# Differential attention ahead of the last keys' norms, and the first mixer's mask in the decay rows

## What is computed

```python
def forgetting_attention(q, k, v, f_logit):
    c = jnp.cumsum(jax.nn.log_sigmoid(f_logit), axis=1)
    ...
        s = jnp.einsum('bhtd,bshd->bhts', qi, k) * scale
        s = s + ci[..., :, None] - c[:, :, None, :]
        s = jnp.where(kpos[None, :] <= qpos[:, None], s, -jnp.inf)
        p = jax.nn.softmax(s, axis=-1)
        return jnp.einsum('bhts,bshd->bthd', p.astype(v.dtype), v)
...
def diff_attention_group(q, k, v, z, q_gain, k_gain, lq1, lk1, lq2, lk2, out_gain, lambda_init):
    q = rmsnorm(q.reshape(b, t, DF_HEADS, 2, DF_HEAD_QK), q_gain) * (DF_HEAD_QK ** -0.5)
    k = rmsnorm(k.reshape(b, t, DF_HEADS, 2, DF_HEAD_QK), k_gain)
    ...
        s = jnp.einsum('bqhcd,bkhcd->bhcqk', q_blk, k).astype(jnp.float32)
        p = jax.nn.softmax(jnp.where(mask, s, neg), axis=-1)
        wts = p[:, :, 0] - lam * p[:, :, 1]
        return jnp.einsum('bhqk,bkhv->bqhv', wts.astype(v.dtype), v)
    ...
    o = rmsnorm(o, out_gain).astype(jnp.float32) * (1.0 - lambda_init)
    return (o * jax.nn.silu(z)).astype(z.dtype)
```

## Time and profile before

| | us |
|---|---|
| median of 3 runs | 921.55 |
| lowest, highest | 918.61, 921.67 |
| the profiled execution | 918.34 |
| its span, first to last instruction | 916.7 |
| TensorE busy | 900.9 |
| VectorE busy | 551.6 |
| ScalarE busy | 292.1 |

### The profile page before, as it was taken

How to read it: one execution, slowest core, us unless ns; L and a number is a source line. 1 busy time by engine, 2 the same in 40 slices (tenths; PEclk the granted TensorE clock), 3 DMA queues, 4 the chain that set the end, 5 groups by cost and what they waited for, 6 DMA issues and landing times.

```text
span 916.7 us, 13260 instructions
## 1 busy us (share of the span) xinstructions
PE 900.9 (98%) x4499; PEld 730.7 (80%) x4499; DVE 551.6 (60%) x968; ACT 292.1 (32%) x596; POOL 72.3 (8%) x138
## 2 busy tenths in 40 slices
PE   8999999999999999999999999999999999999998
PEld 7887776778888888888888888888888897567877
DVE  7247456355877777767743434497777463775654
ACT  6234456523322222222210101443330112454710
POOL 0000000000010010001000001000000000000000
PEclk9999999999999999999999999999999999999999
DMA  8756443254766556655665655578456222212554
GB/s 276 246 188 196 159 128 115 83 160 135 235 200 196 183 190 198 198 193 184 195 198 191 198 184 186 181 224 258 150 149 194 67 86 92 92 62 77 168 194 145
DMA packets 50213, 154.76 MB, mean 169 GB/s; under 512 B 9564, under 2 KB 10860, under 8 KB 50040
## 3 DMA queue, kind: packets, MB, share of 16 engines
q1 hardware_dynamic: 22320, 75.70, 26.1%
q0 software_dynamic: 19008, 69.21, 23.1%
q10 hardware_dynamic: 8840, 9.23, 3.1%
HBM read 149.63 MB, written 4.49 MB: 168 GB/s over the span
## 4 chain that ended last, share of the span: by engine, by line
PE 91%; DVE 3%; issue 2%; DMA 2%; ACT 2%; DVEq 0%; SPq 0%; POOLq 0%; ACTq 0%
PE bank L654 77%; PE bank L713 1%; DMA HI<-wstream 1%; PE bank L1091 1%; PE bank L1071 1%; PE bank L792 1%; PE bank L816 1%; PE bank L1002 1%; PE bank L988 1%; PE bank L806 1%; DVE LO L1621 1%; DMA RAW<-wstream 1%; PE bank L1082 1%; PE bank L795 0%; DVE SQ L1603 0%
## 5 line engine op out<-in xcount | busy, mean ns | idle before, releaser
L654 PE MATMUL bank<-GH,HI 128*128 128x512 f32 (+1 forms) x724 | 292.5, 404 | 1.6 <-issue 1.6
L654 PE MATMUL bank<-GH,LO 128*128 128x512 f32 (+1 forms) x724 | 282.3, 390 | 0.0
L654 PE MATMUL bank<-GL,HI 128*128 128x512 f32 (+1 forms) x724 | 282.0, 389 | 0.0
L1621 DVE TENSOR_TENSOR LO<-RAW,HI 128x1024 fp32r<-128x1024 f32 x88 | 107.5, 1222 | 115.7 <-DMA HI<-wstream 114.8
L654 PEld LDWEIGHTS bank<-GH,HI 128*128 128x128 f32 x724 | 136.5, 188 | 34.1 <-issue 9.0
L654 PEld LDWEIGHTS bank<-GH,LO 128*128 128x128 f32 x724 | 136.3, 188 | 29.0
L654 PEld LDWEIGHTS bank<-GL,HI 128*128 128x128 f32 x724 | 136.8, 189 | 23.9
L636 POOL DMA_DIRECT2D HI<-wstream x132 | 69.8, 529 | 820.2 <-PE bank L654 810.2
L1333 ACT ACTIVATE YC<-AB,PAR 128x512 f32<-128x512 f32 x44 | 36.0, 818 | 140.7 <-DVE AB L1768 140.5
L654 PE MATMUL bank<-AH,HI 128*128 128x512 f32 x176 | 69.3, 394 | 0.0
L654 PE MATMUL bank<-AH,LO 128*128 128x512 f32 x176 | 69.0, 392 | 0.0
(11 more groups left out here) (309 smaller groups left out, 1178.0 us busy)
## 6 DMA issues: line engine op xcount, KB each, us to landing
RAW<-wstream SPq DMA_DIRECT2D x135, 512.0 KB, 3.7
HI<-wstream POOLq DMA_DIRECT2D x132, 512.0 KB, 5.0
X<-x_t SPq DMA_DIRECT2D x8, 256.0 KB, 7.6
NCB<-out_t ACTq DMA_DIRECT2D x4, 512.0 KB, 3.8
out_t<-X ACTq DMA_DIRECT2D x8, 256.0 KB, 5.7
XR<-out_t ACTq DMA_DIRECT2D x8, 256.0 KB, 3.5
out_t<-XR SPq DMA_DIRECT2D x7, 256.0 KB, 3.8
EG<-out_t ACTq DMA_DIRECT2D x1, 1024.0 KB, 6.1
```

What stands on the lines that cost most here:

```text
L654: mm = pe.matmul(out, a, b, start=(first and n == 0), stop=(last and n == 2))
L1621: dve.tensor_tensor(LO[:, u % RING, :], RAW[:, u % RING, :], HI[:, u % RING, :].bitcast(F32), ALU.subtract).then_inc(unit_split, 1)
```

## The change

1. *Mask.* The fourth matmul of the scores goes, with IDF and CSF and ScalarE's two copies that made them. NCB now holds, for each of two heads and two pairs by turns, eight blocks of 128: the transfer lands the four key blocks at places 1, 3, 5, 7 (two transfers of 256 KB a pair, in pieces of 512 bytes), and VectorE writes the block without mask at 0 and blocks with the mask subtracted at 2, 4, 6 (item "bias (p, 0)") and in place at 7 ("bias (p, 1)"). The maxima read a strided choice of these places. The transfer of pair 2 and 3 waits until the maxima of the pair before last are taken.
2. *Order of the first mixer.* Slot 0 stands ahead of the last three quarters of qk 3, slot 1 behind its last quarter, the ring step of that tile behind its remainder (lowqk 3). The new items shift the fills: slots 2, 3, 6, 7, 10 and 11 stand one quarter or two earlier, C 0 and "split 5" ahead of the last quarter of u 2 and qk 6, and lowqk 7 ahead of gate 1.
3. *Order of the second mixer.* X, Y, Z and W of the last blocks stand one eighth earlier. Two eighths of z 0 stand ahead of the last sums, scores 0 behind one more; kn 2 stands in slot 3 behind B 1, kn 3 in slot 4 behind B 2, each with an eighth ahead of it. The list then reads:

```diff
@@ -112,6 +112,16 @@
+def _last_norms(slots):
+
+    slots[0] = [("z", (0, 0)), ("P", 0), QUERIES_KEYS[-1], ("qr", 1)] + slots[0]
+    slots[3].append(("P", 1))
+    slots[3].append(("kn", 2))
+    slots[4].append(("P", 2))
+    slots[4].append(("kn", 3))
+    return slots
...
-            if item[0] in ("A", "B") and item not in without:
+            if item[0] in ("A", "B", "P") and item not in without:
                 order.append(left.pop(0))
-            order.append(item)
+            if item[0] != "P":
+                order.append(item)
...
@@ -195,6 +206,8 @@
+        if n % 4 >= 2 and n < 12:
+            slot.append(("bias", (n // 4 + 1, n % 4 - 2)))
...
-    return (first[:3] + norms[:2] + first[3:4] + [("ncb", 0)] + _merge(first[4:13], norms[2:]) + first[13:] + [("lowqk", 3)]
-            + part(0, 4, products(4, 7)) + part(4, 8, _merge(products(7, 10), scaled))
-            + part(8, 12, [("gelu", 0)] + last[:7] + [("gate", 0)] + last[7:] + [("gate", 1), ("lowqk", 7), ("gate", 2)])
+    return (first[:3] + norms[:2] + first[3:4] + [("ncb", 0)] + _merge(first[4:13], norms[2:]) + first[13:16] + [("bias", (0, 0)), ("bias", (0, 1))] + slots[0][:1] + first[16:18] + slots[0][1:] + first[18:]
+            + _spread([[slots[1][0], ("lowqk", 3)]] + [[x] for x in _flat(slots[1:4])[1:]], products(4, 7)) + part(4, 8, _merge(products(7, 10), scaled))
+            + part(8, 12, [("gelu", 0)] + last[:7] + [("gate", 0)] + last[7:] + [("lowqk", 7), ("gate", 1), ("gate", 2)])
...
-    + _prepare(2, QUERIES_KEYS[43:])
-    + [("qr", 1)] + _eighths(range(1))[:3] + [("kn", 2)] + _eighths(range(1))[3:4] + [("kn", 3)]
-    + _with_products(_attention(4), _eighths(range(5))[4:36], [])
+    + _prepare(2, QUERIES_KEYS[43:-1])
+    + _with_products(_last_norms(_attention(4)), _eighths(range(5))[1:36], [])
...
                         r = slice(64 * e, 64 * e + 64)
-                        pe.matmul(PS[2 + e][:, 0:w], q[r, 4 + p, P * i:P * (i + 1)], k[r, p, 0:w],
-                                  start=(part == 0), stop=False)
-                for e in range(2):
-                    pe.matmul(PS[2 + e][:, P * i:w], IDF[:, :], CSF[:, :], start=False, stop=True).then_inc(s_made, 1)
+                        mm = pe.matmul(PS[2 + e][:, 0:w], q[r, 4 + p, P * i:P * (i + 1)], k[r, p, 0:w],
+                                       start=(part == 0), stop=(part == 2))
+                        if part == 2:
+                            mm.then_inc(s_made, 1)
...
-                    act.dma_start(NCB[:, 2 * n:2 * n + 2, :],
-                                  out_t[2 * n:2 * n + 2, :].unsqueeze(0).to_broadcast([P, 2, T]))\
-                       .then_inc(scratch_landed, 16)
+                    elif n >= 2:
+                        act.wait_ge(max_made, 8 * (n - 1))
+                    for e in range(2):
+                        head = out_t[2 * n + e, :].rearrange("(j c) -> j c", c=P)
+                        act.dma_start(NCB[:, n % 2, e, 1:8:2, :], head.unsqueeze(0).to_broadcast([P, NB, P]))\
+                           .then_inc(scratch_landed, 16)
...
-                dve.wait_ge(scratch_landed, 16 * (n // 4 + 1))
+                S = S.rearrange("p (j c) -> p j c", c=P)
+                bias = NCB[:, n // 4 % 2, e, (slice(2, 3), slice(0, 5, 4), slice(0, 7, 3), slice(1, 8, 2))[n % 4], :]
+                dve.wait_ge(biased, 3 * (n // 4 + 1))
...
+            def mask_bias(p, part):
+
+                rows = NCB[:, p % 2, :, :, :]
+                diagonal = CAUSAL[:, 384:512].unsqueeze(1)
+                if part == 0:
+                    dve.wait_ge(scratch_landed, 32 * (p + 1))
+                    dve.tensor_copy(rows[:, :, 0, :], rows[:, :, 1, :]).then_inc(biased, 1)
+                    dve.tensor_tensor(rows[:, :, 2:7:2, :], rows[:, :, 1:6:2, :],
+                                      diagonal.unsqueeze(1).to_broadcast([P, 2, 3, P]), ALU.subtract).then_inc(biased, 1)
+                else:
+                    dve.tensor_tensor(rows[:, :, 7, :], rows[:, :, 7, :], diagonal.to_broadcast([P, 2, P]), ALU.subtract)\
+                       .then_inc(biased, 1)
```

More of the change, by code:

```diff
@@ L61 @@
 STORED_NCB, STORED_ROWS, STORED_BETA, STORED_NT, STORED_XS = (16 * n for n in (1, 2, 3, 11, 12))
-LANDED_ROWS, LANDED_BETA, LANDED_MS, LANDED_XI = (16 * n for n in (5, 6, 7, 15))
+LANDED_ROWS, LANDED_BETA, LANDED_MS, LANDED_XI = (16 * n for n in (9, 10, 11, 19))
 FREED_VA, FREED_DFV = NB, 2 * NB
@@ L302, in _ring @@
             out.append(("ring", U_KQV + n + RING - 1))
-        if what in ("qk", "u") and n[1] == 3:
+        if (what, n) == ("qk", (3, 3)):
+            continue
+        elif (what, n) == ("lowqk", 3):
+            out.append(("ring", U_QK + 3 + RING - 1))
+        elif what in ("qk", "u") and n[1] == 3:
             out.append(("ring", U_QK + MIX1_UNITS.index((what, n[0])) + RING - 1))
@@ L384, in build @@
         FR = place("FR", [P, 3, T], F32, arena + 64 * KB)
-        NCB = place("NCB", [P, 8, T], F32, arena + 80 * KB)
+        NCB = place("NCB", [P, 2, 2, 8, P], F32, arena + 80 * KB)
         VA = place("VA", [P, NB, 512], F32, arena + 96 * KB)
@@ L389, in build @@
         SGB = place("SGB", [P, 4, P], F32, arena + 112 * KB)
-        IDF = place("IDF", [P, P], F32R, arena + 114 * KB)
-        CSF = place("CSF", [P, P], F32R, arena + 114 * KB + 512)
         assert arena + 115 * KB <= 229368, arena
@@ L1680, in biased_max @@
                 S = PS[2 + e][:, 0:w]
[L1681 removed]
+                S = S.rearrange("p (j c) -> p j c", c=P)
+                bias = NCB[:, n // 4 % 2, e, (slice(2, 3), slice(0, 5, 4), slice(0, 7, 3), slice(1, 8, 2))[n % 4], :]
+                dve.wait_ge(biased, 3 * (n // 4 + 1))
                 dve.wait_ge(s_made, 2 * n + e + 1)
[L1683 removed]
+                dve.tensor_tensor_reduce(S, S, bias, -1.0, 3e38, ALU.add, ALU.min,
                                          MX1[:, c:c + 1]).then_inc(max_made, 1)
+            def mask_bias(p, part):
[9 more added lines that the diff above has]
+                       .then_inc(biased, 1)
             for what, n in MIX1_ORDER:
@@ L1705, in _ @@
                     dve.tensor_tensor(rest, full, top.bitcast(F32), ALU.subtract).then_inc(qk_split, 1)
+                elif what == "bias":
+                    mask_bias(*n)
                 elif what == "A":
```

7 lines of the change are left out of this document (1 added, 6 removed).

## The result

| | us |
|---|---|
| kernel before, median of 20 executions | 917.77 (915.81 to 923.40) |
| changed kernel, median of 20 executions | 921.42 (919.09 to 923.81) |
| ratio, 95% interval | 1.0032 (1.0019 to 1.0044) |
| profiled execution of the changed kernel, its span | 923.08, 921.4 |

The change costs 2.9 us by the ratio (1.7 to 4.0) and 3.65 by the medians, and the forecast was a gain of 1.3. The time itself, 921.42, lies inside the range, yet that is luck: the three runs at hand beforehand stood 3.8 us above the median of twenty.

A forecast was written before the change was run, and what follows sets the result against it. TensorE, busy 98% of the span, was taken as the bound. First mixer -2.6 and second mixer +1.3 summed to -1.3 us: 917.0 for the profiled execution, 920.2 for the three-run median; range 914.6 to 924.5.

The forecast's parts named there:

- VectorE ... has no gap after it: First mixer, slots 8 to 13: VectorE works without idle from about 141.45 us, so slot 12's maxima start at 156.4.
- Rival D: Clock falls more often at new TensorE waits, including ahead of slot 13: slower, 923.3 us with two falls; chance 0.18.
- The 0.95 us of slots 8 to 13: First mixer: slot 12's maxima start at 156.4 instead of 157.40, bringing slot 13's scores 0.95 us earlier, a gain.
- the 1.45 us of slots 0 to 7: First mixer's first eight slots: 2.2 us gained from dropped mask products, less a new 0.75 us wait at slot 1.
- 0.27: First mixer: each dropped pair of mask products saves 0.27 us where TensorE sets the pace; slot 15 counts one such gain.
- slot 9's exponentials don't move with TensorE: First mixer: these start at 139.87 us behind the gelu's table load, and stay there when TensorE runs earlier.
- The second mixer: Start of attention: new waits of 4.1 and 1.3 us at the spreads against 4.2 removed; with new falls, 1.3 us lost.
- the fall at 773: Second mixer, sums of the last key tile: clock at 0.76 over 7 us; avoiding it was credited with 1.7 us.
- 0.3 for new falls: Second mixer: a new wait of 3 to 4 us may bring another clock drop, costing 0.3 us (0 to 1.7).
- B: Second mixer: the spreads don't stall, so all 4.2 us are gained; 914.7 us, chance 0.15.
- C: First mixer: the mask was free and VectorE's added 6.2 us lie on the chain, so no gain; 922.8 us, chance 0.17.
- E: Second mixer: attention starts ahead of the norms only on TensorE's list, ScalarE holding the spreads back; no own time or chance.

The follow-up runs named there:

- experiments 7: Changed kernel with unit 24's ring step behind slot 13's maxima, two gate products ahead of the last sums, both spreads ahead of the first scores: 917.86 us, ratio 0.9993.
- experiment 9: Kernel before with the change's mask and first-mixer order, unit 24's ring step moved behind slot 13's maxima, second mixer as before: 915.46 us, ratio 0.9965.
- 10: Kernel before with the change's first mixer, unit 24's ring step behind slot 13's maxima, and only two gate products ahead of the last sums: 915.39 us, ratio 0.9963.
- experiment 2: Changed kernel with the second mixer's order put back as before, leaving the mask and the first mixer's new order: 919.00 us, ratio 1.0009 to before.
- experiment 5: Changed kernel with only unit 24's ring step on VectorE moved from behind gate 2 to behind slot 13's maxima: 918.10 us, ratio 1.0000 to before.
- 6 before, step moved: Kernel before with only unit 24's ring step on VectorE moved from behind gate 2 to behind slot 13's maxima: 917.18 us, ratio 0.9994.
- experiment 11: Kernel before without the first mixer's pairs of mask products and nothing in their place, so it computes something else: 916.04 us, ratio 0.9972.
- experiment 12: Kernel before with the second mixer's new order, but spread kn 2 behind slot 4 and kn 3 behind slot 6: 922.73 us, ratio 1.0040.
- experiment 1: Kernel before with only the second mixer's new order: 921.20 us against 918.01, ratio 1.0043.
- 4: Kernel before with the change's mask, first mixer's other order left, both bias steps of pair 0 behind the last remainder: 921.89 us, ratio 1.0043.
- 8: Kernel before with the change's first-mixer order, mask products left on TensorE and no bias steps: 917.55 us, ratio 0.9999.

## Why the forecast was wrong, step by step

*The failing step: "VectorE ... has no gap after it", slots 8 to 13.* I added the 1.55 us of bias to VectorE's busy time and took it that nothing else would hold it. The list puts the ring step of unit 24 between gate 2 and slot 12's maxima, and I had counted its work but not its load. Before, that load was issued at 150.30 and landed 4.5 us later, and the step came at 156.26, 1.4 us after the landing. The change brings VectorE to the step at 154.8, while the load, issued when qk 7 ends, moves ahead by 0.6 us only (149.66). An unchanged landing would still have come 0.6 us before the step, so the change didn't make the wait by itself: it took the load's slack from 1.4 us to 0.6, and in this profile the load came 7.0 us after the issue. The issues of the two kernels in the stretch from 145 to 160 us (last number: us to landing), first before, then after:

```profile
HI<-wstream POOLq DMA_DIRECT2D x1, 512.0 KB, 4.5
```

```profile
HI<-wstream POOLq DMA_DIRECT2D x1, 512.0 KB, 7.0
```

In the fourteen profiles it took 4.5 to 7.0 us. In eleven of them, experiments 7, 9 and 10 with the new first mixer included, it took 4.5 to 5.5; the three slow ones are the changed kernel (7.0), experiment 2 (6.8) and experiment 5 (6.0). Only in these three does an instruction-fetch packet of 16 KB, 0.95 us long, fall into the load's way from issue to landing (at 153.6, 153.2 and 152.5 us). So the slow landings go with the fetch; that the fetch causes them is argued from these traces, and no run moves it. What the runs do show is the step's place: moved, the wait and the fall of the clock behind it are gone. Rival D had the place, "the time ahead of slot 13", and its stated price, but not its cause, and I gave it 0.18.

*A second fault, in the sum.* The 0.95 us of slots 8 to 13 came from 157.40 against 156.4, both counted from the start of the span. So it is the whole lead at slot 13, and the 1.45 us of slots 0 to 7 are in it; the sum adds the two. By its own terms the first mixer's gain was 0.95 + 0.27 = 1.2 us and not 2.6, and the whole came to about nothing. The premise behind it, that slot 9's exponentials don't move with TensorE, didn't hold either. They start 1.40 us earlier than the 139.87 of the earlier trace rows, as much as slot 8's scores:

```profile
138.47 0.47 ACT L1305 ACTIVATE P<-bank,SM 128x256 f32<-128x256 f32 x1
```

The distances between the starts of scores show what each stretch gave, in us, without what lies ahead of 70 us:

```text
                              from the product at 70     from slot 8
                              to slot 8                  to slot 15
before                        59.00                      39.99
changed kernel                57.97                      42.78
2 first mixer only            57.97                      42.56
5 changed, step moved         57.97                      38.68
6 before, step moved          58.99                      39.06
9 first mixer, step moved     58.00                      38.67
11 no mask products           57.47                      39.40
```

From slot 8 to slot 15 the forecast has 1.2 us of gain, and the changed kernel loses 2.8. With the step moved it gains 1.3, of which the move alone gives 0.9 in the kernel before, so 0.4 are the change's. With the step in its place and its load in time, slot 12's maxima would start at 154.8 + 1.14 = 155.9, an estimate from the changed kernel's rows: 1.5 us ahead of the earlier trace rows, of which 1.4 stood at slot 8. So even then this term would have been near 0.

*Slots 0 to 7.* Forecast: 2.2 gained, 0.75 lost, net 1.45. Measured 1.03 from the product at 70 us to slot 8: the wait at slot 1 was 0.49, and the pair is worth 0.19 instead of 0.27 (experiment 11), so 1.52 - 0.49. By the Trainium skill, page "TensorE: Matmul & The Clock Gate", section "Back-to-back issue gap", its formula for an isolated matmul makes an estimated 0.11 a pair, which the prediction took; the same section says that this under-counts at small sizes and puts 81 ns on a 128-column matmul in a stream, an estimated 0.16 a pair and 2.6 us for the 32. The distance between the two kernels, 0.19 a pair over eight slots and 2.2 to 2.6 us for the whole, lies close to that second figure, and the row's 0.27 was too much. The pair's row and the next one's were not the whole of what removing the pair changes, so the price of a removal is better read as the distance between two kernels. The bias work was sized well; VectorE's groups in the changed kernel (busy us, mean ns):

```profile
L1708 DVE TENSOR_TENSOR NCB<-NCB,CON 128x768 f32<-128x768 f32 x4 | 3.8, 950 | 0.0
...
L1711 DVE TENSOR_TENSOR NCB<-NCB,CON 128x256 f32<-128x256 f32 x4 | 1.7, 419 | 0.0
L1707 DVE COPY NCB<-NCB 128x256 f32<-128x256 f32 x4 | 1.2, 288 | 0.0
```

That is 1.66 us a pair, 1.4 to 1.5 on the engine as they overlap; 1.55 was said. The maxima with the strided operand take what they took before (0.715 us for 512 columns, 0.713 before): 0% was taken. The landings of the rows now take 3.4 to 7.2 us and none was waited for. The median landing is 4.0 us against 3.8 in the earlier trace rows, the slowest 7.2 against 6.3. The Trainium skill, page "DMA: Bandwidth & Descriptors", section "Specifications", puts full rate at 512 B and above. The decay rows came in 512 packets of 4 KB with a median of 159 ns before, and in 4096 packets of 512 B with a median of 27 ns after, which is 1.36 times the time per byte, so the traces don't bear it out.

*The second mixer.* The new waits were said to be 4.1 us at the first spread and 1.3 at the second; they are 1.07 + 2.74 = 3.8 (the first part taken by the turn ahead of it) and 0.40. The mechanism, RS behind the exponential and the PT copy, is as forecast, and experiment 12 shows that it is that order. The mis-sized term is the clock. I credited 1.7 us for the fall at 773 as if every execution had it; of the 95 of before, 36 have none at all. And I set 0.3 for new falls, while all 50 executions with spreads inside the attention (20 of the changed kernel, 6 of experiment 1, 12 each of experiments 5 and 12) have at least one stretch at half clock, at some 1.6 us each. Forecast 1.3 lost; measured by the medians 3.2 (experiment 1), 2.4 (changed kernel less experiment 2) and 2.6 (experiment 5 less experiment 9), and by the ratios 3.9, 2.1 and 3.2. By the profiles 1.5 us of it are waits. Falls of the clock give about as much again: experiment 5 has 1.5 of them per execution and experiment 9 has 0.6, at some 1.6 us each. Together that is 3.0, and the split is no finer than the medians allow. The profile of experiment 1 also has a wait of 1.86 us for a load on VectorE at 875 us, which costs TensorE 1.51; in the changed kernel's the like wait of 1.74 costs TensorE 0.24. How often it comes stays open.

*The rivals.* B is out: 3.8 us of wait stand there. C is out by its cause, since the products were worth 1.5 us by slot 8; yet its outcome for the first mixer, nothing gained, is what experiment 2 measured (0.8 us lost, -0.7 to 2.5), for another reason. E is out. D is nearest to what happened: two places with a fall beyond the forecast, and 2.9 us lost against its 1.8 for two falls and 3.5 for three. Its condition, idle time ahead of slot 13, was in view, and the row that would have raised its chance is the ring step 1.1 us ahead of the earlier trace rows and the landing of its load.

*The sum, corrected.* By the ratios: first mixer -3.2 with the step moved and +4.0 for the step's place and the clock behind it, second mixer +2.1 to +3.9: +2.9 to +4.7, and measured +2.9 (1.7 to 4.0). The lower end is no check, since the 2.1 was taken from the changed kernel itself; the upper one, from experiment 1 alone, is above the measured interval, but its own runs from 2.4 to 5.5.

## What to carry to other kernels

When a change moves an engine's queue ahead, list each of its items that waits for a transfer, and compare the new arrival with the landing, not with the issue: a load that had landed 1.4 us ahead of its use was left 0.6 us of slack when the engine came 1.5 us sooner and the load's issue only 0.6, and its time to landing varied by 2.5 us between profiles. Put such an item behind the work on which another engine hangs; one moved line turned 919.00 into 915.46. Before terms are added, check that each is a distance over its own stretch: a lead read from the start of the span holds all that was gained ahead of it. And price a stretch at half clock by how many executions have it, since one profile shows it as certain or as absent.

## What the runs showed of the hardware

- The same 512-KB load through GpSimd's queue, issued between 148 and 154 us, took 4.5 to 7.0 us to land in fourteen profiles. In the three with 6.0, 6.8 and 7.0 us an instruction-fetch packet of 16 KB (0.95 us) moves while the load is under way, in the other eleven (4.5 to 5.5 us) none does. That it delays one engine's share of the load was not tested.
- The clock's falls vary between executions of one kernel: of the 95 of before, which has a wait of 1.20 us at 772, 59 have one or more. Of the seven profiles with this wait, four have a fall of 3.41 us close behind it (before, experiments 2, 4 and 8) and three have none (6, 9 and 11).
- The granted clock was near 0.50 for 6.83 us at the waits of 3.27, 3.21 and 3.06 us and, in experiment 12, at a chain of 1.08, 0.99 and 2.00 us; at those of 2.87, 2.74 and 2.73 us it was so for 3.41. So the length of the last wait alone doesn't order them.
